# Neighbourhood attention: adding the skewed bias on TensorE inside each unit's scores instead of keeping a masked bias per head

## The chip, the cores and the metric

The kernel is one program on one core of a Trainium2 chip. The metric is the device time of one execution in microseconds (us). The kernel before was timed in three runs: 3856.1 us in the median, from 3851.97 to 3873.37 us.

The program is written out by hand for five engines: TensorE (PE; PEld is its weight load), VectorE (DVE), ScalarE (ACT), GpSimd (POOL) and SyncE (SP), which issues the DMAs here. Each engine runs its own list in order; semaphores tie the lists together.

## The reference, cut to what matters

The whole reference is two transformer blocks over 512 tokens. The change touches one of its parts, the neighbourhood attention of the first block: 8 heads of 64 columns, 512 latent tokens seen as a grid of 8 rows by 64 columns, and 256 context tokens.

```python
bias = rpb[:, dr[:, None, :, None], dc[None, :, None, :]].astype(f32)
s_win = jnp.einsum('brqhd,brkwhd->bhrqkw', qg, k_band) + bias[None]
s_win = jnp.where(col_ok[:, None, :], s_win, NEG_INF)     # a window of 16 grid columns
s_ctx = jnp.einsum('brqhd,bnhd->bhrqn', qg, kc.astype(f32))
s = jnp.concatenate([s_win.reshape(B, NA_H, rows, GRID_W, n_win), s_ctx], axis=-1)
p = jax.nn.softmax(s, axis=-1)
```

`rpb` holds, for each head, 15 x 31 numbers, looked up by the row distance and the column distance of a query and a key.

## The kernel before, in words

The first block runs through a prelude (norms, and `ADA = 4` of 12 pieces of the modulation product `ada_w`), then the neighbourhood attention (`attention_pe`, `attention_act`, `attention_dve`), then the projections of the recurrence (`z_pe`), and so on. Barriers on all compute engines stand before and after the attention.

**Iterations and units.** The attention has four iterations `i`, one for two heads each. An iteration has 8 units `u`: four tiles of 128 queries (16 grid columns by 8 rows) for each of the two heads. A unit's scores are a bank of 512 columns: 256 window keys (8 rows of 32 grid columns) and 256 context keys. They are kept with the sign turned (queries are scaled by -0.125), so that the softmax takes a minimum. TensorE makes the scores of units 2n and 2n+1 together (`heads_scores_pe`, L633), one head in rows 0 to 63 of the array and one in rows 64 to 127. VectorE then adds the bias to the window half and takes the minimum (L767, L769, L771), ScalarE takes the exponentials (L716, L718), TensorE transposes the weights (L669), ScalarE (even units, L725) or VectorE (odd units, L777) copies them out, TensorE multiplies them by the values (L677), VectorE scales (L787), and the tile is turned and stored (L683, L728, L791).

**Work beside the units.** While iteration i runs, the projections of iteration i+1 (`na_prep_pe`, L812: queries, keys, values, from weights W[0], W[1], W[2] of 512 KB each) are cut into steps of two products. `attention_order` calls for three steps at each unit (`a.rate`). The steps are a generator: a bare `yield` is a step without a product on that engine. The end of the key part is the mark "qk"; at the last unit VectorE reorders queries and keys for iteration i+1 (`na_finish_dve`, L978 and L981).

**The bias.** It is read from a padded table in DRAM by `bias_load`: for each head 8 small DMAs (L344) that write a skewed copy, so that row distance and column distance become plain offsets. The skew comes out with its rows reversed; TensorE multiplies it by a reversed identity (`flip`, `na_bias_pe`, L874) into a bank, and VectorE makes from it three forms for each head (L892), with the columns outside the window set to 1e30. `na.bias` keeps 8 heads x 3 forms x 256 columns. The skewed copies have two buffers, `na.skew[i % 2]`.

**SyncE's list.** For each iteration `na_prep_sp` issues in this order: the three weight loads of i (L903), the 16 small DMAs of `bias_load(i + 1)`, and two `ada_w` pieces of 2 MB each, as two DMAs of 1 MB each (L331). GpSimd multiplies and sums these pieces (`ada_rest_pool`, L514 and L519, eight pieces r0 to r7 in all); a piece's buffer is free when the piece two before it is summed (`ada_summed`). A wait in this list holds everything behind it.

Of the kernel before, what the change touches and what calls it, by code (L numbers as in the profile page):

```python
# [11 lines left out]
ALU = mybir.AluOpType  # L12
# [111 lines left out]
def constants():  # L124
# [5 lines left out]
    c["headones"] = np.kron(np.eye(2), np.ones((64, 64)))  # L130
    c["flip"] = np.eye(P)[::-1]

# [27 lines left out]
    for tile in (0, 1, 3):  # L160
        ci = (NA_SPAN * tile + p % NA_SPAN)[:, None]
        cj = NA_FIRST[tile] + np.arange(NA_KEYS)[None, :]
        c0 = np.clip(ci - 8, 0, 48)
        least.append(np.where((cj >= c0) & (cj < c0 + 16), -FAR, FAR))
    c["na_least"] = np.concatenate(least, 1)
# [49 lines left out]
def memory(k, A, PS):  # L215
# [25 lines left out]
    na.skew = [A.take(2, GH * NA_WIDE) for _ in range(2)]  # L241
    na.bias, na.least = A.take(8, 3 * GH * NA_KEYS), A.take(3, NA_KEYS)
    m2 = A.at
# [91 lines left out]
def bias_load(k, p, i):  # L335

    S, na = k.S, k.na
    for x in range(2):
        if i >= 2:
            p.wait_ge(S.bias_filled, 2 * (i - 2) + x)  # L340
        for y in range(GH):
            row = k.scratch[2 * i + x, y:y + GH, 0:NA_WIDE]
            skew = bass.AP(tensor=row.tensor, offset=row.offset + 64 - NA_SPAN, ap=[[1, NA_SPAN], [160, GH], [1, NA_WIDE]])
            p.e.dma_start(na.skew[i % 2][NA_SPAN * y:NA_SPAN * y + NA_SPAN, x].rearrange("p (a b) -> p a b", b=NA_WIDE),  # L344
                          skew).then_inc(*p.up(S.landed(f"bias{i}"), (x, y)))
# [279 lines left out]
def heads_scores_pe(k, p, a, i, units, first):  # L625

    S = k.S
    p.wait_ge(S.qk_ready, (a.name, i))
    for u in (first, first + 1):
        p.claim(("bank", a.scores[u % 2]), S.weights_exp, (a.name, i, u))  # L630
    for j in range(2):
        for u in (first, first + 1):
            ins = p.e.matmul(k.bank[a.scores[u % 2]][:, TC * j:TC * j + TC], units[u][3], units[u][4][j], start=True, stop=True,  # L633
                             skip_group_check=True)
            if j:
                ins.then_inc(*p.up(S.scores_filled, (a.name, i, u)))


def attention_pe(k, p, a):
# [3 lines left out]
    for i in range(a.n):  # L643
        work = Work(a.prep_pe(k, p, a, i + 1) if i + 1 < a.n else None)
        units = a.units(i)
        for step, u in attention_order(a):
# [10 lines left out]
            if step == "values":  # L657
                a.values_pe(k, p, a, i)
                continue
            tile, c0, w, _, _, va, _ = units[u]  # L660
            if step == "scores":
# [71 lines left out]
def attention_dve(k, p, a):  # L733
# [4 lines left out]
    for i in range(a.n):  # L738
        work = Work(a.prep_dve(k, p, a, i + 1) if i + 1 < a.n else None)
        units = a.units(i)  # L740
        for step, u in attention_order(a):
# [13 lines left out]
            if step == "values":  # L755
                continue
            tile, c0, w, _, _, _, bias = units[u]
            cols = a.small[:, u % 4, :]
            low = cols[:, 0:1]
            if step == "scores":  # L760
                s, ps = a.S[u % 2], k.bank[a.scores[u % 2]]
                old = before(a, i, u, 2)
                if old:
                    p.wait_ge(S.weights_filled, old)
                p.in_order()
                p.wait_ge(S.scores_filled, key)
                p.e.tensor_tensor_reduce(out=s[:, 0:TC], in0=ps[:, 0:TC], in1=bias, scale=1.0, scalar=FAR, op0=ALU.add,  # L767
                                         op1=ALU.min, accum_out=low).then_inc(*p.up(S.scores_biased, key))
# [97 lines left out]

def na_bias_pe(k, p, i):

    S, na = k.S, k.na
    p.wait_ge(S.landed(f"bias{i}"), (1, GH - 1))  # L870
    for x in range(2):
        h = 2 * i + x
        p.claim(("bank", 6 + x), S.bias_kept, h)
        p.e.matmul(k.bank[6 + x][:, 0:GH * NA_WIDE], k.K["flip"], na.skew[i % 2][:, x], start=True, stop=True,  # L874
                   skip_group_check=True).then_inc(*p.up(S.bias_filled, h))
        yield
        yield


def na_bias_dve(k, p, i):  # L880

    S, na = k.S, k.na
    for x in range(2):
        h = 2 * i + x
        yield
        yield
        p.wait_ge(S.bias_filled, h)
        skewed = k.bank[6 + x][:, 0:GH * NA_WIDE].rearrange("p (a b) -> p a b", b=NA_WIDE)
        kept = na.bias[:, h].rearrange("p (v a b) -> p v a b", a=GH, b=NA_KEYS)
        for tile in (0, 1, 3):  # L890
            v, at = NA_FORM[tile], NA_FIRST[tile] - NA_SPAN * tile + NA_SPAN
            p.e.scalar_tensor_tensor(out=kept[:, v], in0=skewed[:, :, at:at + NA_KEYS], scalar=-1.0,  # L892
                                     in1=na.least[:, v, None, :].to_broadcast([P, GH, NA_KEYS]), op0=ALU.mult, op1=ALU.max).then_inc(
                                         *(p.up(S.bias_kept, h) if tile == 3 else p.up(S.vector_step)))


NA_COLUMNS = (1152, 1664, 2176)
# [16 lines left out]
def na_prep_pe(k, p, a, i):  # L914
    S = k.S
    for j in range(3):
# [10 lines left out]
        if j == 1:  # L927
            yield from na_bias_pe(k, p, i)
            yield "qk"


def na_prep_act(k, p, a, i):
    S = k.S
    for j, dst in enumerate((a.q_n, a.k_n, a.v_f)):
# [19 lines left out]
        if j == 1:  # L954
            for _ in range(4):
                yield
            yield "qk"


def na_prep_dve(k, p, a, i):  # L960
    S = k.S
    for j in range(3):
# [7 lines left out]
        if j == 1:  # L970
            yield from na_bias_dve(k, p, i)
            yield "qk"
# [11 lines left out]
def na_columns(x, tile):  # L984

    return x.rearrange("p (r c) -> p r c", c=GW)[:, :, NA_FIRST[tile]:NA_FIRST[tile] + NA_KEYS]


# [21 lines left out]
def na_setup(k):  # L1010
# [4 lines left out]
    def units(i):  # L1015
        return [(tile, 64 * h, 64, a.q_s[64 * h:64 * h + 64, tile * P:tile * P + P],
                 [na_columns(a.k_s[64 * h:64 * h + 64, 0:T], tile), a.k_s[64 * h:64 * h + 64, T:TK]],
                 lambda j, h=h, tile=tile: a.v_t[:, 2 * tile + j if j < 2 else 6 + j, 64 * h:64 * h + 64],
                 a.bias[:, 2 * i + h, NA_FORM[tile] * TC:NA_FORM[tile] * TC + TC]) for tile in range(TT) for h in range(2)]
    two_heads(a, units)  # L1020
# [3196 lines left out]
```

## Time and profile before

| | |
|---|---|
| median of three runs | 3856.1 us |
| profiled execution, its own time | 3852.21 us |
| its span in the trace | 3850.4 us |
| PE busy | 3280.3 us, 85% of the span |
| DVE busy | 2121.7 us, 55% |
| POOL busy | 1384.7 us, 36% |
| ACT busy | 764.9 us, 20% |
| DMA moved | 831.77 MB |

The profile page is one execution. The attention stands between about 99 us and 291 us of the span, and the projections for its first iteration between 66 and 99 us. PE records come in two for each product in 32-bit floats, so an x12 is six products; a row of the timeline gives start, length, and in square brackets how long the engine was idle before it and for whom. The granted clock is given as a share of the full one. A transpose and a product both show as MATMUL.

### The profile page before, as it was taken

The page shows a single profiled execution, that of the slowest core. Times are in us where ns is not written, and L with a number is a line of the kernel's source. Part 1 is how long each engine was busy: PE and PEld are TensorE (multiplying, and loading weights), DVE is VectorE, ACT ScalarE, POOL GpSimd, SP SyncE. Part 2 cuts the span into 40 slices and gives each one's busy share as a digit, 9 for nine tenths or more (in the row PEclk, how much of TensorE's full clock was granted, in tenths as well). Part 3 has the DMA queues.
Part 4 walks back from the last instruction along what each step waited for, and adds up shares of the span by engine and source line. Part 5 has one row for each costly group of instructions (what it writes and reads, how often), then busy time and mean ns, then how long its engine had stood idle before and what let it go on. Part 6 is the DMA issues. An engine that isn't in the chain of part 4 may idle for free. (4 is left out here: it accounts for less than half of the span.)

```text
span 3850.4 us, 39434 instructions
## 1 busy us (share of the span) xinstructions
PE 3280.3 (85%) x14438; PEld 2437.0 (63%) x14438; DVE 2121.7 (55%) x4234; ACT 764.9 (20%) x1791; POOL 1384.7 (36%) x1218
## 2 busy tenths in 40 slices
PE   8889888887677978647788888889897999999999
PEld 3566478775233535326567776667785778887787
DVE  2341345548889888867777668776653320133201
ACT  2231233222111111112420012320013210122100
POOL 0930022105677777754355546545500000000000
PEclk9998899998888989878689999889998999999999
DMA  6412100017999999987689999889941134431342
GB/s 206 129 66 82 31 1 1 13 44 275 363 368 373 373 374 384 393 308 276 208 288 376 394 377 371 302 282 392 394 145 34 60 125 150 147 99 61 126 152 100
DMA packets 424598, 831.77 MB, mean 216 GB/s; under 512 B 40467, under 2 KB 266830, under 8 KB 424398
## 3 DMA queue, kind: packets, MB, share of 16 engines
q0 software_dynamic: 147456, 536.94, 37.2%
q1 hardware_dynamic: 276950, 292.31, 23.3%
q8 instruction: 116, 1.90, 0.2%
q14 instruction: 76, 0.62, 0.0%
HBM read 826.98 MB, written 2.17 MB: 215 GB/s over the span
## 5 line engine op out<-in xcount | busy, mean ns | idle before, releaser
L2828 PE MATMUL banks<-arena 128*128 128x256 f32 (+1 forms) x4992 | 1142.4, 388 | 74.4 <-DMA arena<-in_l_w_up 30.4
L2828 PEld LDWEIGHTS banks<-arena 128*128 128x128 f32 (+1 forms) x4992 | 965.4, 195 | 236.8 <-issue 36.2
L2375 POOL DMA_INDIRECT arena<-in_peer_u,arena x512 | 577.6, 1128 | 456.4 <-DVE arena L2505 175.4
L2375 POOL DMA_INDIRECT arena<-in_peer_v,arena x512 | 590.5, 1153 | 400.5 <-DVE arena L2491 242.3
L2505 DVE CUSTOM_DVE_ANT_0 arena<-arena 128x1024 f32<-128x1024 f32 x512 | 628.1, 1227 | 104.4 <-DMA arena<-in_peer_u,arena 86.4
L2447 PE MATMUL banks<-arena 128*128 128x512 f32 x768 | 415.5, 685 | 188.5 <-ACT arena L2466 123.6
L2491 DVE SCALAR_TENSOR_TENSOR arena<-arena 128x1024 f32<-128x1024 f32 x316 | 406.3, 1286 | 29.4 <-DMA arena<-in_peer_v,arena 18.7
L2447 PEld LDWEIGHTS banks<-arena 128*128 128x128 f32 x768 | 159.7, 218 | 401.1 <-issue 246.4
L3737 PE MATMUL banks<-arena 128*128 128x256 f32 x1408 | 310.5, 378 | 0.0
L3786 DVE TENSOR_TENSOR arena<-banks,arena 128x512 f32<-128x512 f32 x44 | 30.5, 692 | 504.9 <-PE banks L2828 504.6
L3737 PEld LDWEIGHTS banks<-arena 128*128 128x128 f32 x1408 | 265.7, 189 | 38.3
L3758 ACT ACTIVATE arena<-banks 128x512 f32<-128x512 f32 x44 | 26.3, 597 | 684.7 <-PE banks L2828 679.7
L3279 DVE CUSTOM_DVE_ANT_0 arena<-banks,arena 128x256 f32<-128x256 f32 (+3 forms) x128 | 59.8, 467 | 138.6 <-PE banks L3161 131.4
L2140 PE MATMUL banks<-arena 128*128 128x512 f32 (+1 forms) x320 | 126.0, 542 | 9.4 <-DMA arena<-in_peer_q_w 5.9
L1632 POOL TENSOR_TENSOR arena<-arena 128x512 f32<-128x512 f32 x48 | 52.4, 1091 | 223.5 <-DVE arena L1598 119.1
L552 PE MATMUL banks<-arena 128*128 128x512 f32 (+1 forms) x336 | 132.1, 553 | 0.0
L812 PE MATMUL banks<-arena 128*128 128x512 f32 (+1 forms) x320 | 120.2, 525 | 5.7 <-ACT arena L455 3.6
L1552 ACT ACTIVATE arena<-banks 128x512 f32<-128x512 f32 x132 | 77.0, 597 | 223.9 <-PE banks L1428 173.2
L3231 ACT ACTIVATE arena<-arena 128x256 f32<-128x256 f32 (+3 forms) x128 | 69.3, 542 | 254.2 <-DVE arena L3279 185.0
L3202 PE MATMUL banks<-arena 128*128 128x64 f32 (+1 forms) x720 | 117.0, 296 | 1.5 <-ACT arena L3249 1.5
L3202 PEld LDWEIGHTS banks<-arena 128*128 128x128 f32 x720 | 111.8, 224 | 4.5 <-issue 2.6
L1435 PE MATMUL banks<-arena 128*128 128x128 f32 x960 | 114.5, 278 | 0.0
(341 smaller groups left out, 3883.7 us busy)
## 6 DMA issues: line engine op xcount, KB each, us to landing
arena<-in_l_w_gate SPq DMA_DIRECT2D x44, 1024.0 KB, 5.5
arena<-in_l_w_up SPq DMA_DIRECT2D x44, 1024.0 KB, 6.1
arena<-in_l_w_down SPq DMA_DIRECT2D x44, 1024.0 KB, 5.1
arena<-in_ada_w SPq DMA_DIRECT2D x24, 1024.0 KB, 7.6
arena<-in_l_w_qkv SPq DMA_DIRECT2D x24, 1024.0 KB, 6.4
arena<-in_w_in SPq DMA_DIRECT2D x33, 512.0 KB, 4.1
arena<-in_l_w_out SPq DMA_DIRECT2D x16, 1024.0 KB, 5.4
arena<-in_peer_q_w SPq DMA_DIRECT2D x10, 1024.0 KB, 12.4
```

Of the source, the lines that this page charges most:

```text
L552: ins = p.e.matmul(k.bank[b][0:m, 0:n], k.W[slot][:, c, 0:m], rhs(c), start=c == 0, stop=c == c_n - 1, skip_group_check=True)
L812: ins = p.e.matmul(k.bank[b][0:m, 0:n], k.W[slot][:, c, 0:m], rhs(c), start=c == 0, stop=c == c_n - 1, skip_group_check=True)
L1435: ins = p.e.matmul(bank[:, s * P:s * P + P], left[:, s, :], right[:, s, :], start=True, stop=True, skip_group_check=True)
L1552: p.e.activation(flat(dst), chunk_bank(k, B, c, step), ACT.Copy).then_inc(*p.up(S.chunk_copied, (c, name)))
L2140: ins = p.e.matmul(k.bank[4][:, cols], ws[:, c, P * j:P * j + P], k.HT[:, c, cols], start=c == 0, stop=c == DC - 1, skip_group_check=True)
L2375: p.e.indirect_dma_start(e.ring[slot], None, tables[table], bass.IndirectOffsetOnAxis(ap=e.IDX[h][:, t, j:j + 1], axis=0)).then_inc(*p.up( ...
L2447: ins = p.e.matmul(k.bank[b], e.diag[x % 4], e.ring[slot][:, half * T:half * T + T], start=h == 0 and j == 0, stop=h == HEADS - 1 and j == ...
L2491: p.e.scalar_tensor_tensor(out=e.ACC[t], in0=e.ring[slot], scalar=factor, in1=e.ACC[t], op0=ALU.mult, op1=ALU.add).then_inc(*p.up(S.rows_a ...
L2505: p.e.tensor_tensor_reduce(out=e.prod, in0=e.ring[slot], in1=e.H2[:, t, :], scale=1.0, scalar=0.0, op0=ALU.mult, op1=ALU.add, accum_out=e. ...
L2828: ins = p.e.matmul(out, left(c), right(c), start=c == 0, stop=c == c_n - 1, skip_group_check=True)
L3202: ins = p.e.matmul(k.bank[5][:, 0:x.w], a.PT[u % 2][:, j * P:j * P + P], values, start=j == 0, stop=j == len(x.values) - 1, skip_group_che ...
L3737: ins = p.e.matmul(k.bank[4 + o // 2][:, o % 2 * TH:o % 2 * TH + TH], w[:, r, P * o:P * o + P], a.hid[:, (i - 1) % 2, TH * r:TH * r + TH], ...
```

## The change

The forms kept for each head go away, with `na_bias_pe` and `na_bias_dve`. The skewed copy is multiplied by the reversed identity once for each unit, and TensorE adds the result in the bank that holds the unit's scores: after the four score products of a pair, two products of 128x256 (L637 of the changed kernel) read the columns of the skew that the tile's form wants. `flip` gets a minus sign since the scores have theirs turned. The first score product of a bank begins it (`start=j == 0`), the flip ends it. What VectorE adds now is a mask of three forms (0 inside the window, 1e30 outside), spread over the 8 rows, the same for all heads; it is loaded as 128 x 768 numbers where 128 x 96 were.

A skewed copy is now read until the last unit of its iteration has its scores, and `bias_load` waits for that.

```diff
@@ bias_load (SyncE)
         if i >= 2:
-            p.wait_ge(S.bias_filled, 2 * (i - 2) + x)
+            p.wait_ge(S.scores_filled, ("na", i - 2, 6 + x))
@@ memory
-    na.bias, na.least = A.take(8, 3 * GH * NA_KEYS), A.take(3, NA_KEYS)
+    na.least = A.take(3, GH * NA_KEYS)
@@ heads_scores_pe
     for j in range(2):
         for u in (first, first + 1):
-            ins = p.e.matmul(k.bank[a.scores[u % 2]][:, TC * j:TC * j + TC], units[u][3], units[u][4][j], start=True, stop=True,
-                             skip_group_check=True)
-            if j:
-                ins.then_inc(*p.up(S.scores_filled, (a.name, i, u)))
+            p.e.matmul(k.bank[a.scores[u % 2]][:, TC * j:TC * j + TC], units[u][3], units[u][4][j], start=j == 0, stop=False,
+                       skip_group_check=True)
+    p.wait_ge(S.landed(f"bias{i}"), (1, GH - 1))
+    for u in (first, first + 1):
+        p.e.matmul(k.bank[a.scores[u % 2]][:, 0:TC], k.K["flip"], units[u][7], start=False, stop=True,
+                   skip_group_check=True).then_inc(*p.up(S.scores_filled, (a.name, i, u)))
@@ na_prep_pe
         if j == 1:
-            yield from na_bias_pe(k, p, i)
             yield "qk"
@@ na_prep_act
-            for _ in range(4):
-                yield
@@ na_prep_dve
-            yield from na_bias_dve(k, p, i)
```

The list of an engine changes in two places that matter here. The first is PE between the third pair of scores of iteration 0 and the first scores of iteration 1. L812 is a projection product, L633 a score product, L874 the flip before; the waits are the semaphores' names. Before:

```order
L633 MATMUL banks<-arena 128x256 x3
L669 MATMUL banks<-arena 128x128 x4
L677 MATMUL banks<-arena 128x64 [waits output_scaled,act_weights]
L677 MATMUL banks<-arena 128x64 x3
L683 MATMUL banks<-arena 128x128
L874 MATMUL banks<-arena 128x384 [waits dve_emptied,landed_bias1]
L874 MATMUL banks<-arena 128x384 [waits dve_emptied]
L669 MATMUL banks<-arena 128x128 [waits weights_exp]
```

and, further on, the last unit with what follows it:

```order
L669 MATMUL banks<-arena 128x128 [waits weights_exp]
L669 MATMUL banks<-arena 128x128 x3
L677 MATMUL banks<-arena 128x64 [waits output_scaled,act_weights]
L677 MATMUL banks<-arena 128x64 x3
L683 MATMUL banks<-arena 128x128 [waits dve_stored]
L812 MATMUL banks<-arena 128x256 x2
L677 MATMUL banks<-arena 128x64 [waits output_scaled,dve_weights]
```

The same last unit in the changed kernel (L671 is the old L669, L679 the old L677, L685 the old L683), and the first scores of iteration 1 with their flips:

```order
L671 MATMUL banks<-arena 128x128 [waits weights_exp]
L671 MATMUL banks<-arena 128x128 x3
L679 MATMUL banks<-arena 128x64 [waits output_scaled,act_weights]
L679 MATMUL banks<-arena 128x64 x3
L685 MATMUL banks<-arena 128x128 [waits dve_stored]
L679 MATMUL banks<-arena 128x64 [waits output_scaled,dve_weights]
L679 MATMUL banks<-arena 128x64 x3
L685 MATMUL banks<-arena 128x128 [waits act_stored,output_scaled]
L633 MATMUL banks<-arena 128x256 [waits qk_ready]
L633 MATMUL banks<-arena 128x256 x3
L637 MATMUL banks<-arena 128x256 [waits landed_bias1]
L637 MATMUL banks<-arena 128x256
```

The four empty or flip steps are gone from the projections, so these come four steps earlier; no projection is left beside the last unit.

The second place is SyncE's list from the weights of iteration 1 to those of iteration 2. Before:

```order
L903 DMA arena<-in_w_in 128x8x128 [waits proj_filled] x3
L344 DMA arena<-rpb_padded 16x8x48 [waits bias_filled]
L344 DMA arena<-rpb_padded 16x8x48 x7
L344 DMA arena<-rpb_padded 16x8x48 [waits bias_filled]
L344 DMA arena<-rpb_padded 16x8x48 x7
L331 DMA arena<-in_ada_w 128x4x512 [waits ada_summed]
L331 DMA arena<-in_ada_w 128x4x512
L331 DMA arena<-in_ada_w 128x4x512 [waits ada_summed]
L331 DMA arena<-in_ada_w 128x4x512
L903 DMA arena<-in_w_in 128x8x128 [waits proj_filled] x3
```

The changed kernel (L875 is the old L903):

```order
L875 DMA arena<-in_w_in 128x8x128 [waits proj_filled] x3
L344 DMA arena<-rpb_padded 16x8x48 [waits scores_filled]
L344 DMA arena<-rpb_padded 16x8x48 x7
L344 DMA arena<-rpb_padded 16x8x48 [waits scores_filled]
L344 DMA arena<-rpb_padded 16x8x48 x7
L331 DMA arena<-in_ada_w 128x4x512 [waits ada_summed]
L331 DMA arena<-in_ada_w 128x4x512
L331 DMA arena<-in_ada_w 128x4x512 [waits ada_summed]
L331 DMA arena<-in_ada_w 128x4x512
L875 DMA arena<-in_w_in 128x8x128 [waits proj_filled] x3
```

The order is the same; what the small DMAs wait for is another signal. The same stands once more an iteration later.

## Rows read from the trace of the kernel before

**Rows 1.** Busy time of each engine in iterations 0 to 3; PEclk, DMA share, GB/s.

```profile
99.50:157.00 57.50, 48.63 (x228) 30.57 (x228) 24.16 (x71) 15.88 (x48) 56.64 (x18) 0.97 0.42 120
157.00:209.00 52.00, 48.31 (x229) 31.09 (x228) 19.40 (x72) 14.59 (x47) 35.42 (x13) 0.97 0.34 107
209.00:260.20 51.20, 46.62 (x227) 29.99 (x226) 19.39 (x72) 14.59 (x47) 30.58 (x10) 1.00 0.33 113
260.20:291.30 31.10, 23.11 (x144) 18.58 (x143) 15.69 (x63) 12.17 (x41) 0.00 (x0) 0.82 0.06 16
```

**Rows 2.** PE by line, 99 to 291 us: busy, mean ns; idle before, for whom.

```profile
L812 PE MATMUL banks<-arena 128*128 128x256 f32 x96 | 23.1, 382 | 0.0
L874 PE MATMUL banks<-arena 128*128 128x384 f32 x12 | 5.2, 512 | 5.4 <-DVE arena L969 5.4
```

**Rows 3.** Timeline of PE, prologue and the passage to iteration 0.

```profile
66.13 20.35 PE L812 MATMUL banks<-arena 128*128 128x512 f32 x48 [3.57 <-ACT arena L455]
86.32 1.66 PE L874 MATMUL banks<-arena 128*128 128x384 f32 x4
88.40 10.58 PE L812 MATMUL banks<-arena 128*128 128x512 f32 x32 [0.42 <-DVE arena L892]
...
155.20 1.08 PE L677 MATMUL banks<-arena 128*128 128x64 f32 x8 [2.89 <-DVE arena L787]
```

**Rows 4.** Timeline of PE in iteration 2.

```profile
208.95 1.14 PE L633 MATMUL banks<-arena 64*128 64x256 f32 x8
...
213.89 5.40 PE L812 MATMUL banks<-arena 128*128 128x512 f32 x12 [0.57 <-ACT arena L836]
...
244.64 1.15 PE L633 MATMUL banks<-arena 64*128 64x256 f32 x8
...
257.66 1.03 PE L812 MATMUL banks<-arena 128*128 128x256 f32 x4
```

**Rows 5.** Timeline of PE in iteration 3, third pair.

```profile
272.83 1.63 PE L633 MATMUL banks<-arena 64*128 64x256 f32 x8 [1.03 <-ACT arena L718]
```

**Rows 6.** Timeline of SyncE's DMA issues, 99 to 164 us.

```profile
99.42 7.79 SPq L344 DMA_DIRECT2D arena<-rpb_padded  x16
115.11 16.42 SPq L331 DMA_DIRECT2D arena<-in_ada_w  x4
131.58 21.13 SPq L903 DMA_DIRECT2D arena<-in_w_in  x3
152.76 8.29 SPq L344 DMA_DIRECT2D arena<-rpb_padded  x16
161.09 2.32 SPq L331 DMA_DIRECT2D arena<-in_ada_w  x4
```

**Rows 7.** L903 alone, 130 to 150 us: two issues, from issue to landing.

```profile
DMA to landing us min/median/max: 8.9/9.4/9.9
```

**Rows 8.** Busy time, clock and DMA of two stretches, columns as in Rows 1.

```profile
163.00:175.60 12.60, 12.60 (x45) 6.24 (x44) 0.76 (x3) 1.59 (x4) 9.29 (x3) 1.00 1.03 368
66.00:72.00 6.00, 5.87 (x7) 2.53 (x8) 0.31 (x1) 2.00 (x5) 0.00 (x0) 0.50 1.05 389
```

**Rows 9.** Timeline of POOL: begin of the sums of r2 and r4, end of r7.

```profile
130.56 7.16 POOL L514 TENSOR_TENSOR arena<-arena 128x2048 f32<-128x2048 f32 x2
...
166.23 7.16 POOL L514 TENSOR_TENSOR arena<-arena 128x2048 f32<-128x2048 f32 x2 [4.26 <-DMA arena<-in_ada_w]
...
237.22 8.31 POOL L519 TENSOR_TENSOR arena<-arena 128x2048 f32<-128x2048 f32 x3
```

**Rows 10.** DVE: duration ns min/median/max, first and last start, of L978 and L981.

```profile
L978 DVE COPY arena<-arena x4: 416/420/2239, 89.2 to 254.1; 128x512 f32<-128x512 f32 x4
L981 DVE COPY arena<-arena x4: 562/564/3842, 89.6 to 254.5; 128x768 f32<-128x768 f32 x4
```

**Rows 11.** Timeline of DVE at the end of iteration 0.

```profile
147.71 2.24 DVE L978 COPY arena<-arena 128x512 f32<-128x512 f32 x1
...
153.74 0.68 DVE L777 COPY arena<-banks 128x512 f32<-128x512 f32 x1
```

More of the change, by code:

```diff
@@ L130, in constants @@
     c["headones"] = np.kron(np.eye(2), np.ones((64, 64)))
-    c["flip"] = np.eye(P)[::-1]
+    c["flip"] = -np.eye(P)[::-1]
     rot = np.zeros((P, P))
@@ L163, in constants @@
         c0 = np.clip(ci - 8, 0, 48)
-        least.append(np.where((cj >= c0) & (cj < c0 + 16), -FAR, FAR))
+        least.append(np.tile(np.where((cj >= c0) & (cj < c0 + 16), 0.0, FAR), (1, GH)))
     c["na_least"] = np.concatenate(least, 1)
@@ L659, in attention_pe @@
                 continue
-            tile, c0, w, _, _, va, _ = units[u]
+            tile, c0, w, _, _, va, _, _ = units[u]
             if step == "scores":
@@ L756, in attention_dve @@
                 continue
-            tile, c0, w, _, _, _, bias = units[u]
+            tile, c0, w, _, _, _, least, _ = units[u]
             cols = a.small[:, u % 4, :]
@@ L766, in attention_dve @@
                 p.wait_ge(S.scores_filled, key)
-                p.e.tensor_tensor_reduce(out=s[:, 0:TC], in0=ps[:, 0:TC], in1=bias, scale=1.0, scalar=FAR, op0=ALU.add,
+                p.e.tensor_tensor_reduce(out=s[:, 0:TC], in0=ps[:, 0:TC], in1=least, scale=1.0, scalar=FAR, op0=ALU.add,
                                          op1=ALU.min, accum_out=low).then_inc(*p.up(S.scores_biased, key))
@@ L861, in rotary_dve @@
     p.e.tensor_tensor(parts[1][0:m, :], k.bank[b][0:m, 0:n], sin[0:m, 0:n], ALU.mult).then_inc(*p.up(k.S.rotated, key))
[L867 to L875, printed above, removed]
-        yield
[L877 to L894, printed above, removed]
 NA_COLUMNS = (1152, 1664, 2176)
@@ L954, in na_prep_act @@
         if j == 1:
-            for _ in range(4):
-                yield
             yield "qk"
@@ L986, in na_columns, with na_skewed @@
     return x.rearrange("p (r c) -> p r c", c=GW)[:, :, NA_FIRST[tile]:NA_FIRST[tile] + NA_KEYS]
+def na_skewed(x, tile):
+    at = NA_FIRST[tile] - NA_SPAN * tile + NA_SPAN
+    return x.rearrange("p (a b) -> p a b", b=NA_WIDE)[:, :, at:at + NA_KEYS]
 NA_VALUES = (7, 6, 7)
@@ L1018, in units @@
                  lambda j, h=h, tile=tile: a.v_t[:, 2 * tile + j if j < 2 else 6 + j, 64 * h:64 * h + 64],
-                 a.bias[:, 2 * i + h, NA_FORM[tile] * TC:NA_FORM[tile] * TC + TC]) for tile in range(TT) for h in range(2)]
+                 a.least[:, NA_FORM[tile], :], na_skewed(a.skew[i % 2][:, h], tile)) for tile in range(TT) for h in range(2)]
     two_heads(a, units)
```

## The prediction

> **What bounds the kernel now.** I read first where the changed lines run, 66 to 291 us, and then the busy time of each engine in the four iterations [rows 1]. In iterations 0 to 2 PE is busy 46.6 to 48.6 us of 51.2 to 57.5 us, VectorE 19.4 to 24.2 us: PE's list sets the pace. In iteration 3, which has no projections beside it, PE is busy 23 of 31 us, and the chain scores, minimum, exponential, transpose sets it. POOL ends its sums at 245.5 us [rows 9], 46 us before the attention does, so it has slack. Barriers stand on both sides, and what follows begins from there, so I count a microsecond in the attention as one in the whole. Next I read the idle times in PE's timeline [rows 3 to 5], and last SyncE's list with its times [rows 6], since the edit of one wait stands there.
>
> **Removed.** In the prologue two flips of 384 columns, 1.66 us, and PE's idle 0.42 us behind the VectorE work on them [rows 3]: -2.1 us. In each of iterations 0 to 2 two flips: 12 records took 5.2 us in all, 1.7 us an iteration, and PE stood idle 5.4 us for VectorE's copy L969 in front of the second, 1.8 us an iteration [rows 2]: -3.5 us. The 24 instructions of L892 stand on VectorE, which isn't the pace; beyond the idle just counted they are worth nothing.
>
> **Added on PE.** 32 flips of 256 columns. The trace has a full product of that size: 96 records, 48 products, 23.1 us, so 0.48 us with its share of the edges, some 0.46 us in a row [rows 2]. A pair of scores takes 1.14 us for four products [rows 4], 0.29 us each, but those run two heads beside each other, and the flip uses all 128 rows. Bounds 0.29 us and 0.83 us (a flip of 384 columns in the prologue, half of 1.66 us [rows 3]); I take 0.46, since that row has the size itself. At the start of an iteration PE waits for the exponentials of unit 0 anyway, and only the first flip is ahead of these: +0.46 us. The other three pairs: +0.92 us each. That is 3.2 us an iteration, against the 3.5 us removed.
>
> At the end of an iteration the projections that filled the last unit are gone (the rows of order above). Before, two of them (1.03 us) stood between the transposes of unit 7 and its output [rows 4]. VectorE's copy of unit 7 takes 0.68 us and stands behind L978 and L981, in the best case 0.98 us together [rows 10, 11]. I get PE waiting about 1.0 us there (0 to 2). So iterations 0 to 2 get -3.5 + 3.2 + 1.0 = +0.7 us each, +2.1 us in all.
>
> In iteration 3 the flips lie on the chain: PE waits 1.0 us for the exponentials (L718) in front of the pair [rows 5]. 0.46 to 0.92 us for the first pair, 0.92 us for the others: +3.4 us.
>
> **The wait that moved.** This is the largest term. Before, `bias_load(2)` found its signal there when SyncE came to it, at 99.42 us [rows 6]. Now it waits for the scores of unit 6 of iteration 0, which come in the fourth pair. Queued behind it are the two `ada_w` pieces and the three weight loads of iteration 2, which PE needs from the first unit of iteration 1. Let F be the time of that signal.
>
> From F: the 16 small issues take about 7.9 us (7.79 and 8.29 us [rows 6]). The next two pieces were 16.4 us apart from first to last issue before, since the second waited for POOL; now both are free, as at 161.09 us, where four issues took 2.3 us. So 4.2 MB go out in a row, with the weights behind them. The trace has that traffic: from 163.0 to 175.6 us, 12.6 us at 368 GB/s, four halves and one weight load issued from 161.09 us on [rows 6, 8]. The DMAs of the weights at 131.58 us, behind 2.1 MB, landed 8.9 to 9.9 us after their issue [rows 7]; 2.1 MB more at 389 GB/s [rows 8] is 5.4 us. Both give about 15 us from the first piece's issue to the landing of W[0]. In sum F + 0.2 + 7.9 + 15.0 = F + 23.1 us.
>
> PE wants W[0] sooner. In iteration 2 the first projection came 4.9 us after the iteration's start and the fourth pair 35.7 us after it [rows 4]. In the changed list six more products of 512 columns (0.90 us each, as the six of 5.40 us [rows 4]) and two of 256 stand ahead of the fourth pair, +6.3 us, the old flips and their wait don't, -3.5 us, and the flips of three pairs do, +2.3 us: the fourth pair at 40.8 us, and after its four products and one flip F at 42.4 us. The iteration ends at 52.0 us (51.3 + 0.7) and the next projection comes 4.9 + 0.46 us later, at 57.4 us: F + 15.0 us. PE stands 23.1 - 15.0, some 8.0 us. It does so in iteration 1 (for the weights of iteration 2) and, the pattern being the same, in iteration 2: +16.0 us. Bounds for one: 5 us (each issue and transfer at its fastest) to 10 us.
>
> A rule of the Trainium skill bears on it. The row first: two weight loads issued behind 2.1 MB took 9.4 us, about what 2.6 MB take plus a start. "DMA: Bandwidth & Descriptors", in "Queues, rings and completion order", says that SyncE owns one row of rings, and that each DMA engine consumes the descriptors of its ring in order. By it the weights can't pass the 4.2 MB, and the stall is 8 us; if they could, it would be none. The trace agrees with the rule.
>
> **The clock.** After PE's idle 3.57 us the granted clock was 0.50 (1.2 GHz of 2.4) from 66 to 72 us with PE busy 5.87 us of 6.0 [rows 3, 8]: that is 3 us of work lost. An idle of 8 us should have at least one such stretch behind it: +3.0 us for each stall (1.7 to 5), +6.0 us.
>
> **VectorE against POOL.** At the end of iteration 0, L978 and L981 took 2.24 and 3.84 us, elsewhere 0.42 and 0.56 us [rows 10, 11]. POOL's sums ran without a break then, and none ran at the end of iteration 2, where POOL was done at 245.5 us, nor at that of iteration 1 (POOL is busy 35.4 of its 52.0 us [rows 1]). PE paid with an idle of 2.89 us [rows 3] and a slower start of iteration 1; the iteration took 57.5 us where its cold start explains 3.1 us over the 51.3 us of iteration 2. I put the price at 3.8 us. In the changed kernel iteration 0 begins at 97.4 us, its F is at 97.4 + 3.1 + 42.4 = 143 us, r2 is issued at 151 us instead of 115.1 [rows 6] and can't be summed before 156 us, while L978 comes at about 149 us and r1's sum ended at 130.6 [rows 9]: POOL is idle there, -3.8 us. But the whole chain of sums moves too. With F now that of iteration 1: r4 lands at F + 13, each sum takes 15.5 us (7.2 + 8.3 [rows 9]), r7 runs from F + 60 to F + 75; iteration 2 begins at F + 10, has a stall and its clock (11 us), and comes to its L978 at F + 69. So the collision comes back there, with less cover on PE: +5.0 us (0 to 7). POOL ends about F + 75, iteration 3 about F + 110, so POOL stays off the path.
>
> The skill's "SBUF — State Buffer", in "Who interferes with whom", says that a VectorE copy in a 2-port mode and a GpSimd instruction exclude each other for the whole instruction. By it L978 waits out whatever instruction POOL has begun, and the price is what the row shows; the trace agrees, and without the rule the +5.0 and -3.8 us would both be nothing.
>
> **The mask.** 344 KB more to load in the prelude, 0.9 us at 389 GB/s, beside PE work that waits for no DMA there: 0 (up to +1).
>
> **The sum.** -2.1 + 2.1 + 3.4 + 16.0 + 6.0 - 3.8 + 5.0 = +26.6 us. The profiled execution took 3852.2 us (its span 3850.4, and 1.8 around it): 3878.8 us. The median of the runs is 3.9 us above that execution, within the scatter of three runs, so I forecast 3879 us.
>
> **The rivals.** *The loads are in time.* If W[0] lands within 15 us of F, because the 16 issues or the transfers are faster than I read, or the weights don't queue behind the pieces, both stalls and their clock go: 26.6 - 22.0 = +4.6, without the collision of iteration 2 about 0: 3852 to 3857 us. Rows 7 speak against it. *Faster than before.* The place is the flip: at 0.29 us instead of 0.46 (what a score product costs in a pair), the 32 give back some 5 us, and with loads in time and no second collision the sum is -5 to -7 us: 3846 us. It decides where PE can put a flip beside a score product of the other head's rows; the full 128 rows speak against it. *The stalls are dearer.* If the clock stays at half for twice the stretch after an idle of 8 us, or the skew of the next iteration lands late as well (it is due at about F + 10.5, its first reader comes at F + 10.9), each stall costs 15 to 18 us: 3890 to 3900 us.
>
> **Chances.** The forecast's mechanism 0.70, by itself 3870 to 3888 us; loads in time 0.17; faster than before 0.04; dearer 0.09. The range that holds 8 in 10 reaches down into the second case and up to the start of the last: 3854 to 3890 us. About 0.5%, 19 us, is what a measurement of this kernel can tell from no change. The forecast lies 23 to 27 us above before, close to that bound, and a fifth of its own case falls within it. Slower by over 0.5%: 0.66. Within: 0.31. Faster by over 0.5%: 0.03.
>
> **What the changed profile would show.** PE idle before the first projection (L814) of iterations 1 and 2, for DMA of the weights, about 8 us each; POOL's r2 starting near 155 us instead of 130.6; SyncE's small DMAs starting at 142 to 143 us instead of 99.4; L637 at 0.46 us each; L946 and L949 (the old L978 and L981) fast at the end of iteration 0, slow at that of iteration 2; the attention ending at about 317 us instead of 291. The prediction is wrong if PE has no such idle, or if later parts of the kernel take the 26 us back.

## The result, and the profile after

The changed kernel took 3881.6 us in the median of 19 runs (3872.96 to 3897.28), the kernel before 3861.9 us in the 19 beside them. The ratio is 1.0058, with a 95% interval from 1.0045 to 1.0071: 17 to 27 us slower. The forecast was 3879 us and the range 3854 to 3890 us. The sum behind it, +26.6 us, stood on one execution of 3852.2 us, 9.7 us under the median that the kernel before shows here.

The profiled execution of the changed kernel took 3891.2 us, its span is 3889.4 us. PE's first product behind the attention (L528) starts at 318.93 us in it, and at 291.29 us in the trace before: the attention ends 27.6 us later. The other 11 us of difference between the two spans lie behind it. That part took 3559.1 us before, 3570.5 us here, and between 3556.9 and 3577.7 us in the ten experiments, whatever they changed in the attention; one execution can't tell more. So below I compare the attention by its traces, and whole kernels by their timed ratios.

Iterations 0 to 3 of the changed kernel, with the columns of [rows 1]:

```profile
97.80:154.90 57.10, 52.14 (x238) 33.55 (x238) 17.11 (x65) 15.89 (x48) 30.55 (x10) 0.94 0.10 23
154.90:218.10 63.20, 52.83 (x240) 34.45 (x239) 17.30 (x66) 14.61 (x47) 30.58 (x10) 0.91 0.34 101
218.10:285.90 67.80, 54.90 (x239) 35.73 (x238) 21.05 (x66) 14.61 (x47) 61.34 (x20) 0.85 0.51 163
285.90:318.90 33.00, 25.85 (x159) 20.61 (x158) 15.68 (x63) 12.07 (x41) 0.00 (x0) 0.86 0.00 1
```

VectorE has some 2 us less to do in an iteration (17.3 us where 19.4 stood), and it gains nothing by it. Iterations 1 and 2, 52.0 and 51.2 us long before, are 63.2 and 67.8 us. The granted clock is lower too: 0.91 and 0.85 where 0.97 and 1.00 stood. SyncE's list, which answers to [rows 6]:

```profile
76.63 21.05 SPq L875 DMA_DIRECT2D arena<-in_w_in  x3
144.63 7.44 SPq L344 DMA_DIRECT2D arena<-rpb_padded  x16
152.12 2.30 SPq L331 DMA_DIRECT2D arena<-in_ada_w  x4
154.46 12.21 SPq L875 DMA_DIRECT2D arena<-in_w_in  x3
207.21 7.68 SPq L344 DMA_DIRECT2D arena<-rpb_padded  x16
214.93 2.33 SPq L331 DMA_DIRECT2D arena<-in_ada_w  x4
217.31 12.18 SPq L875 DMA_DIRECT2D arena<-in_w_in  x3
```

Nothing is issued between 97.7 us and 144.6 us. Before, the same 16 small DMAs went out at 99.4 us. Then all of it comes at once, in two bursts. PE's timeline shows what the weights at the end of each burst do to it:

```profile
154.54 0.48 PE L685 MATMUL banks<-arena 128*128 128x128 f32 x1 [0.45 <-DVE arena L789]
154.95 2.08 PE L633 MATMUL banks<-arena 64*128 64x256 f32 x8
156.96 1.59 PE L637 MATMUL banks<-arena 128*128 128x256 f32 x4
...
168.70 6.82 PE L814 MATMUL banks<-arena 128*128 128x512 f32 x12 [7.37 <-DMA arena<-in_w_in]
...
231.46 7.86 PE L814 MATMUL banks<-arena 128*128 128x512 f32 x12 [6.90 <-DMA arena<-in_w_in]
...
283.15 1.94 PE L679 MATMUL banks<-arena 128*128 128x64 f32 x8 [4.72 <-DVE arena L789]
```

Two idles for the weights, 14.3 us together; behind them six products that take 6.82 and 7.86 us instead of 5.40 us [rows 4]; and an idle of 4.7 us for VectorE at the end of iteration 2, which stood at the end of iteration 0 before (2.89 us [rows 3]). The last is VectorE's copies beside GpSimd's sum of r7 (they took 0.42 and 0.56 us in the median of the same kernel's four). VectorE's timeline, and GpSimd's under it (r4's first instruction and r7's last three):

```profile
277.00 2.15 DVE L946 COPY arena<-arena 128x512 f32<-128x512 f32 x1
279.18 2.58 DVE L949 COPY arena<-arena 128x768 f32<-128x768 f32 x1
```

```profile
220.21 3.60 POOL L514 TENSOR_TENSOR arena<-arena 128x2048 f32<-128x2048 f32 x1 [31.34 <-DMA arena<-in_ada_w]
...
274.33 8.55 POOL L519 TENSOR_TENSOR arena<-arena 128x2048 f32<-128x2048 f32 x3
```

GpSimd waited 31 us for r4 and was still summing r7 when the copies came. The flips themselves cost what a full product of their size costs, 0.38 us a record, two records each (the largest group of the page has 0.39 us). The line's own view, with the duration in ns as least, median and most:

```profile
L637 PE MATMUL banks<-arena x64: 381/381/794, 98.9 to 308.6; 128*128 128x256 f32 x64
```

### The profile page after: what moved, and what is told of

Same layout as the page of the kernel before. It is cut to its first block and busy times, and to the rows that moved or that the text cites. A ratio compares the mean times of both kernels' runs of the same rounds, so it can differ in the third digit from the quotient of the medians.

```text
span 3889.4 us, 39502 instructions
## 1 busy us (share of the span) xinstructions
PE 3299.4 (85%) x14486; PEld 2454.1 (63%) x14486; DVE 2112.2 (54%) x4210; ACT 765.6 (20%) x1791; POOL 1386.9 (36%) x1218
## 5 line engine op out<-in xcount | busy, mean ns | idle before, releaser
L2349 POOL DMA_INDIRECT arena<-in_peer_u,arena x512 | 591.3, 1155 | 455.1 <-DVE arena L2479 163.6
L2349 POOL DMA_INDIRECT arena<-in_peer_v,arena x512 | 579.1, 1131 | 406.5 <-DVE arena L2465 244.2
L814 PE MATMUL banks<-arena 128*128 128x512 f32 (+1 forms) x320 | 124.1, 541 | 18.4 <-DMA arena<-in_w_in 14.3
```

The source lines that it names most:

```text
L814: ins = p.e.matmul(k.bank[b][0:m, 0:n], k.W[slot][:, c, 0:m], rhs(c), start=c == 0, stop=c == c_n - 1, skip_group_check=True)
L2349: p.e.indirect_dma_start(e.ring[slot], None, tables[table], bass.IndirectOffsetOnAxis(ap=e.IDX[h][:, t, j:j + 1], axis=0)).then_inc(*p.up( ...
```

## The experiments

Each table row gives the start of the first scores, the length of iterations 0 to 3 (from scores to scores, the last one to L528) and L528's start, in us. All are one profiled execution; the ratio to before is timed.

| kernel | start | 0 | 1 | 2 | 3 | end | ratio (95%) |
|---|---|---|---|---|---|---|---|
| before | 99.5 | 57.5 | 52.0 | 51.3 | 31.1 | 291.3 | |
| changed | 97.8 | 57.2 | 63.1 | 67.9 | 33.0 | 318.9 | 1.0058 (1.0045 to 1.0071) |
| e1 four skews | 97.3 | 63.0 | 54.6 | 54.2 | 34.1 | 303.1 | 1.0024 (1.0007 to 1.0041) |
| e2 wait only | 100.4 | 54.4 | 57.9 | 61.2 | 30.9 | 304.8 | 1.0026 (1.0013 to 1.0040) |
| e3 weights first | 96.9 | 56.1 | 54.4 | 59.1 | 33.0 | 299.5 | 1.0013 (0.9998 to 1.0027) |
| e4 busy stall | 96.9 | 57.0 | 61.3 | 68.4 | 32.7 | 316.3 | one run, 3882.7 us |
| e5 steps kept | 96.7 | 57.5 | 52.1 | 52.1 | 32.6 | 290.8 | 0.9983 (0.9968 to 0.9998) |
| e6 ScalarE reorders, steps kept | 99.4 | 57.5 | 52.1 | 52.1 | 33.3 | 294.3 | 0.9987 (0.9970 to 1.0004) |
| e7 no flips | 96.6 | 58.5 | 52.2 | 52.2 | 34.7 | 294.1 | 0.9980 (0.9964 to 0.9997) |
| e8 before, ScalarE reorders | 101.8 | 55.6 | 56.0 | 51.3 | 30.3 | 294.9 | 0.9983 (0.9969 to 0.9998) |
| e9 bias later, steps kept | 97.4 | 57.5 | 53.8 | 53.8 | 31.5 | 293.9 | 0.9987 (0.9975 to 0.9999) |
| e10 ScalarE in the loop | 97.6 | 55.2 | 52.1 | 53.8 | 31.6 | 290.1 | 1.0006 (0.9991 to 1.0021) |

The diffs are cut to the lines that matter; of e3, e5, e6, e9 and e10 the rest is said in words. The theory was the prediction's: the moved wait holds back the weights (the stalls and the clock behind them) and shifts GpSimd's sums. The main rival was that the flips on PE are the cost.

**e1, take the wait away.** Four skewed copies, one for each iteration, fit in what the old forms left free.

```diff
-    na.skew = [A.take(2, GH * NA_WIDE) for _ in range(2)]
+    na.skew = [A.take(2, GH * NA_WIDE) for _ in range(4)]
@@ bias_load
-        if i >= 2:
-            p.wait_ge(S.scores_filled, ("na", i - 2, 6 + x))
```

> The changed kernel with a skewed copy for each of the four iterations, so that SyncE's list waits for no scores. Theory (the moved wait holds the weights back): PE has no idle for the DMA of the weights in iterations 1 and 2 (14.3 us less), and its clock doesn't fall there; SyncE's and GpSimd's times are those of the kernel before, so the collision of VectorE's two copies with GpSimd is again at the end of iteration 0, not of iteration 2. The attention ends at 295 to 298 us of the span (291 before, 319 changed); the time is 1.001 to 1.002 of before. Rival (the flips on PE and the emptied last unit are the cost): the attention ends at 310 us or later and the time is 1.005 of before.

The idles for the weights are gone, iterations 1 and 2 are 8.6 and 13.6 us shorter, and the attention ends 15.8 us sooner. That is the theory, and not the rival's 310 us. But the end is 303.1 us, 5 us above the latest that I expected; the ratio, 1.0024, is just above the expected 1.001 to 1.002, which its interval covers. The collision stands again in iteration 0, and it costs more than the kernel before paid, since no projection covers the last unit. VectorE's timeline, then PE's, of this kernel:

```profile
149.09 2.25 DVE L944 COPY arena<-arena 128x512 f32<-128x512 f32 x1
151.38 4.74 DVE L947 COPY arena<-arena 128x768 f32<-128x768 f32 x1
```

```profile
157.50 1.94 PE L677 MATMUL banks<-arena 128*128 128x64 f32 x8 [6.99 <-DVE arena L787]
...
212.92 1.08 PE L677 MATMUL banks<-arena 128*128 128x64 f32 x8 [0.98 <-DVE arena L787]
...
214.85 2.08 PE L631 MATMUL banks<-arena 64*128 64x256 f32 x8
```

The other half of the miss is in the last two lines, from the end of iteration 1 with no collision at all: PE idles 0.98 us, and then the first pair of iteration 2 runs at half the clock (2.08 us for 1.14). Iterations 1 and 2 are 54.4 us, where I had 52.0.

**e2, the wait alone, in the kernel before.**

```diff
@@ bias_load, in the kernel before
-            p.wait_ge(S.bias_filled, 2 * (i - 2) + x)
+            p.wait_ge(S.scores_filled, ("na", i - 2, 6 + x))
```

> The kernel before with one line changed: bias_load waits for the scores of unit 6 and 7 instead of for the old flip. Theory: the stall is the time from that signal F to the landing of the weights (23.1 us by the prediction) less the time from F to PE's first projection of the next iteration. Here the fourth pair comes 35.7 us into an iteration, F at 36.8 us and the next projection at 56.2 us, F + 19.4 us, so the stall is only 3.7 us, with some 2 to 3 us of clock, twice, and the collision with GpSimd moves from iteration 0 to iteration 2. The attention ends at 301 to 306 us. Rival (the wait costs what it costs in the changed kernel, about 22 us, whatever stands ahead of it): 313 us.

SyncE's timeline, then PE's:

```profile
140.30 7.42 SPq L344 DMA_DIRECT2D arena<-rpb_padded  x16
147.77 2.63 SPq L331 DMA_DIRECT2D arena<-in_ada_w  x4
150.44 11.80 SPq L903 DMA_DIRECT2D arena<-in_w_in  x3
```

```profile
164.24 7.46 PE L812 MATMUL banks<-arena 128*128 128x512 f32 x12 [5.14 <-DMA arena<-in_w_in]
...
220.93 8.12 PE L812 MATMUL banks<-arena 128*128 128x512 f32 x12 [3.92 <-DMA arena<-in_w_in]
...
271.08 1.94 PE L677 MATMUL banks<-arena 128*128 128x64 f32 x8 [2.63 <-DVE arena L787]
```

The end at 304.8 us is within what was expected. One line of the diff, alone, makes the kernel slower: 13.5 us in the attention. The idles are 5.1 and 3.9 us (3.7 expected), less than in the changed kernel, because the fourth pair of scores comes sooner in the old order. From the first small DMA to PE's first product with the weights it is 23.9 and 22.7 us here, and 24.1 and 24.3 us in the changed kernel: nearly the same in both, as the theory has it. Iteration 0 is 3.1 us shorter than before and iteration 2 pays the collision instead.

**e3, the same wait, another order behind it.** SyncE issues the three weight loads of iteration i+1 between the small DMAs and the two pieces.

```diff
     if i + 1 < a.n:
         bias_load(k, p, i + 1)
+    if 1 <= i and i + 1 < a.n:
+        na_weights_sp(k, p, i + 1)
     for r in (2 * i, 2 * i + 1):
         ada_rest_sp(k, p, r)
```

> The changed kernel with SyncE issuing the weights of iteration i+1 behind the small DMAs but ahead of the two ada_w pieces. Theory (the weights stand in the queue behind 4.2 MB): they land 0.2 + 7.9 + 4.4 = 12.5 us after F, PE wants them at F + 15, so both stalls go and with them the clock; GpSimd's sums stay late, so the collision stays at the end of iteration 2. The attention ends at 297 to 301 us. Rival (the 16 small issues and the late start are what counts, and the order of the transfers is not): at least half of the 14.3 us of idle stays and the attention ends at 308 us or later.

SyncE's timeline, then PE's:

```profile
142.63 7.44 SPq L344 DMA_DIRECT2D arena<-rpb_padded  x16
150.11 2.69 SPq L875 DMA_DIRECT2D arena<-in_w_in  x3
```

```profile
159.98 5.40 PE L814 MATMUL banks<-arena 128*128 128x512 f32 x12 [0.57 <-ACT arena L838]
...
263.66 1.94 PE L679 MATMUL banks<-arena 128*128 128x64 f32 x8 [4.69 <-DVE arena L789]
```

The end is 299.5 us, as expected. The list still stands until 142.6 us, the 16 small issues still come first, but the weights don't follow 4.2 MB. The first load landed 7.0 us after its issue, 14.5 us after the first small DMA; PE reached it 17.4 us after that DMA and didn't wait. So a stall needs both, the wait and the large transfers between it and the weights. The collision in iteration 2 remains, since GpSimd's pieces are as late as in the changed kernel.

**e4, PE kept busy in the stall.** Eight products more, into the bank of the first projection, ahead of PE's wait for the weights.

```diff
+        if j == 0 and i >= 2:
+            p.claim(("bank", na_bank(0, 0)), S.act_emptied, ("na", i, 0, 0))
+            for x in range(8):
+                p.e.matmul(k.bank[na_bank(0, 0)][:, 0:T], k.ones, k.HT[:, x, :], start=True, stop=True, skip_group_check=True)
         p.wait_ge(S.landed(f"w{j}"), ("na", i))
```

> The changed kernel with 8 products of 128x512 more in iterations 1 and 2, into the bank of the first projection and ahead of PE's wait for the weights; their result is overwritten. They take about 7 us and stand where PE was idle 7.4 and 6.9 us. Theory (the stall costs its length and the clock behind it): the idle falls to under 1 us, the end of the stall doesn't move, and the six products behind it take 5.4 us each time instead of 6.82 and 7.86 us: the attention ends 3 to 4 us sooner, at 315 us. Rival (the clock behind the stall comes from something else, as the wait for VectorE at the end of the iteration): the six products take as long as before and the end stays at 319 us.

PE's timeline; L892 are the products added:

```profile
160.91 7.15 PE L892 MATMUL banks<-arena 128*128 128x512 f32 x16 [0.47 <-ACT arena L838]
167.89 5.32 PE L814 MATMUL banks<-arena 128*128 128x512 f32 x12
...
222.07 7.15 PE L892 MATMUL banks<-arena 128*128 128x512 f32 x16 [0.47 <-ACT arena L838]
229.13 5.43 PE L814 MATMUL banks<-arena 128*128 128x512 f32 x12
```

With PE busy, the six products behind take 5.32 and 5.43 us instead of 6.82 and 7.86: the clock behind the stall is the stall's doing, and it costs 1.5 and 2.4 us, read from one execution. Iteration 1 is 1.8 us shorter, the end 316.3 us (0.9 us of which is the earlier start). It is 1.3 us later than expected; the collision at the end of iteration 2 was worse in this run (an idle of 7.2 us instead of 4.7).

**e5, the emptied unit filled again.** Four skews, and the four bare steps of the old bias work kept in the sequence of projections, on PE, ScalarE and VectorE.

```diff
         if j == 1:
+            for _ in range(4 if i else 0):
+                yield
             yield "qk"
```

> The changed kernel with four skewed copies (no wait for scores) and with the four bare steps of the old bias work kept in the projections' sequence of iterations 1 to 3, on all engines, so that PE again has six plus two products beside unit 7. With the steps gone (the kernel with four skews alone) iterations 1 and 2 took 54.6 and 54.2 us, and PE's clock was at half for 3.4 us at the start of each. Theory (PE's idle at the emptied unit 7 costs its length and brings the clock down): iterations 1 and 2 take 51.5 to 52.5 us, the first pair of scores of iteration 2 takes 1.14 us and not 2.08, and the attention ends at 293 to 296 us. Rival (the clock falls because of the flips themselves): 53.5 us or more, and the first pair stays at 2.08 us.

PE's timeline at the end of iteration 1 and the start of iteration 2:

```profile
203.63 1.03 PE L812 MATMUL banks<-arena 128*128 128x256 f32 x4
204.50 1.00 PE L677 MATMUL banks<-arena 128*128 128x64 f32 x8
...
206.21 1.15 PE L631 MATMUL banks<-arena 64*128 64x256 f32 x8
...
211.79 5.40 PE L812 MATMUL banks<-arena 128*128 128x512 f32 x12 [0.56 <-ACT arena L836]
```

Two products stand again ahead of the last unit's output, PE doesn't idle there, and all first pairs take 1.14 us. Iterations 1 and 2 are 52.1 us, 2.5 and 2.1 us less than in e1; the attention ends at 290.8 us, 12.3 us ahead of e1 and 2 us earlier than I expected. Of the 12.3 us, 5.5 us are iteration 0's, where the two products cover a part of the collision. Against the changed kernel it is 28.1 us shorter in the traces, and the two ratios to before lie 0.75% apart. Against before it can't be called faster: its attention ends only 0.5 us sooner, where the ratio of 0.9983 would ask for 6.6 us. The four kernels timed together, e5 to e8, have ratios from 0.9980 to 0.9987 while their attentions end between 290.8 and 294.9 us, so a part of these ratios is likely the common runs of before, and not the kernels.

**e6, ScalarE reorders queries and keys.** e5 with VectorE's two copies moved to ScalarE (`na_finish_act`), the one before iteration 0 too. e8 is the same edit in the kernel before.

```diff
-    p.e.tensor_copy(a.k_s, a.k_n).then_inc(*p.up(S.qk_ready, ("na", i)))
+    p.e.activation(a.k_s, a.k_n, ACT.Copy).then_inc(*p.up(S.qk_ready, ("na", i)))
```

> As the kernel with four skews and the steps kept, and ScalarE instead of VectorE reorders queries and keys at the end of an iteration, so that no copy of VectorE from SBUF to SBUF stands beside GpSimd's sums. Theory (that collision costs 4 to 7 us wherever it falls): PE has no idle over 1 us for VectorE in front of the outputs of any iteration, iteration 0 takes 53 to 54.5 us, and the attention ends at 287 to 290 us, ahead of the kernel before (291.3). The time is 0.999 of before. Rival (the copies were slow for another reason, as PE's or the DMA's traffic, or ScalarE is later with its own work): ScalarE's copies are slow or delay the exponentials, and the end stays at 293 us or later.

> The kernel before with ScalarE instead of VectorE reordering queries and keys. Theory (the collision of iteration 0 costs the kernel before 3.8 us): iteration 0 takes 53.7 to 54.5 us instead of 57.5, iteration 1 loses its 0.7 us, the attention ends at 287 to 288 us, and the time is 0.999 of before. Rival: ScalarE's copies take 0.6 and 0.9 us on a path that VectorE's took 0.4 and 0.6 us on, and iterations 1 and 2 get longer by a microsecond each, so that the end is at 289 to 290 us.

Both miss, and e6 ends where its rival had it. No long idle for VectorE is left in either, as the theory says, but the first scores come 2.7 and 2.3 us later (ScalarE's two copies of 0.6 and 0.8 us stand in front of them, behind its other work), and in e6 the clock fell once more in iteration 0, so that it took 57.5 us all the same. e8 lost 4 us in iteration 1, where its trace has the clock at half at 162 and 193 us. The ends are 294.3 and 294.9 us. The timed ratio of e8, 0.9983, doesn't show the 3.6 us (0.1%) that its trace lost.

**e7, the price of the flips.** e1 without them; the bias is left out of the scores.

> The kernel with four skews without its flips: the bias is left out of the scores, everything else stays. It prices the 32 products on PE. Theory (PE is the pace, each flip costs its time, 0.99 us for a pair): iterations 1 and 2 take 3.0 to 3.9 us less than 54.6 and 54.2 us, iteration 3 some 3 us less, and the attention ends at 289 to 292 us instead of 303.1. Rival (flips stand where PE waits anyway): less than 5 us in all, 298 us or later.

Iterations 1 and 2 are 2.4 and 2.0 us shorter than in e1, and the end is 294.1 us: 9.0 us for 32 flips, 0.28 us each (0.8 us of the 9.0 is an earlier start, and iteration 0 has 4.4 us of it). It is less than 0.46 us, and less than the 11 to 14 us that I expected. The place where it is missing is iteration 3: without the flips it is 34.7 us, longer than e1's 34.1, and three of its four pairs of scores take 2.08 us, half the clock, where e1 has one. That less work on PE brought this about is my reading; no run tests it. The rival's bound of 5 us is passed, but the flips are not worth their whole time.

**e9, the order of the list instead of the memory.** The changed kernel's two skewed copies and its wait, with the small DMAs of iteration i behind the weights of iteration i, and the steps kept.

```diff
 def na_prep_sp(k, p, a, i):
     ...
-    if i + 1 < a.n:
-        bias_load(k, p, i + 1)
+    if i:
+        bias_load(k, p, i)
```

> The changed kernel with its two skewed copies and its wait for the scores, but the small DMAs of iteration i issued behind the weights of iteration i instead of ahead of them (one place later in SyncE's list), and the four bare steps kept. Theory (it was what stood behind the waiting DMAs that cost, not the wait and not the number of buffers): no idle of PE for the weights, the attention ends within 1.5 us of the kernel with four skews and the steps kept, at 290 to 292 us, and the time is 0.998 to 1.000 of before. Rival (two buffers are too few: the skew lands too late for the first flip of its iteration, or GpSimd's pieces are late again): an idle in front of the flips, or the collision in iteration 2 as well, and an end at 295 us or later.

SyncE's timeline, to be read beside [rows 6]:

```profile
113.00 16.43 SPq L331 DMA_DIRECT2D arena<-in_ada_w  x4
129.47 22.90 SPq L875 DMA_DIRECT2D arena<-in_w_in  x3
152.42 8.73 SPq L344 DMA_DIRECT2D arena<-rpb_padded  x16
161.19 2.53 SPq L331 DMA_DIRECT2D arena<-in_ada_w  x4
```

No stall, neither for weights nor in front of a flip, and SyncE's times are within 2.2 us of those of before: the wait is harmless where nothing urgent stands behind it. The end is 293.9 us, 1.9 us above what I expected: iterations 1 and 2 each had a stretch of half clock (53.8 us instead of 52.1). The ratio is 0.9987.

**e10, ScalarE in the loop only.** e5 with the reordering on ScalarE at the end of iterations 0 to 2, and on VectorE before iteration 0.

> Four skews, the steps kept, and ScalarE reordering queries and keys at the end of iterations 0 to 2 only; before iteration 0 VectorE does it, since ScalarE's two copies put 2 us in front of the first scores when it did that one too. Theory (the collision of VectorE's copies with GpSimd costs iteration 0 some 2.3 us where PE has cover): iteration 0 takes 55 to 55.5 us instead of 57.5, the first scores come at 97 us, and the attention ends at 288 to 289 us, the earliest of all. Rival (iteration 0 is slow for its cold start alone): it takes 57 us or more and the end is at 290.5 us or later.

Iteration 0 is 55.2 us as expected, 2.3 us less than in e5. The collision costs that much where a cover stands, and 6.9 us where none does (e1's iteration 0 against e3's). Iteration 2 met a stretch of half clock from 211.3 us on and took 53.8 us, so the end is 290.1 us instead of 288 to 289. Its line, to be read beside the 5.40 us of e5:

```profile
210.37 7.09 PE L812 MATMUL banks<-arena 128*128 128x512 f32 x12 [0.57 <-ACT arena L836]
```

Its ratio is 1.0006: it can't be told from e5 or from before.

## Why the prediction was right

The lengths of the iterations answer to the terms one by one. Actual against predicted change:

| | predicted | measured |
|---|---|---|
| prologue (earlier start) | -2.1 | -1.7 |
| iteration 0: collision gone, tail and flips | -3.1 + 0.7 = -2.4 | -0.4 |
| iteration 1: stall, clock, tail and flips, less the slow start of before | 8.0 + 3.0 + 0.7 - 0.7 = +11.0 | +11.2 |
| iteration 2: the same and the collision | 8.0 + 3.0 + 0.7 + 5.0 = +16.7 | +16.6 |
| iteration 3: flips on the chain | +3.4 | +1.9 |
| sum | +26.6 | +27.6 |

The time itself is within 3 us of the forecast, and a part of that is luck. The traces have the attention 27.6 us longer, where the sum said 26.6; the timed difference is 17 to 27 us, near whose upper end both lie; and the base of 3852.2 us was 9.7 us low. From the median of 19 runs the same sum would have given 3888.5 us, still in the range but 6.9 us too high.

*The wait that moved.* Right, in place and mechanism (e2 has the wait alone; e3 and e9 keep it and remove its stall by order, e1 takes it away by memory), and the number of skewed buffers was not the matter. Both halves of the difference of 8 us were 1 to 2.5 us too small: the weights came 24.1 and 24.3 us after the first small DMA (22.9 by the sum), PE wanted them 16.7 and 17.4 us after it (14.8), since the iteration's end and its slow start took longer than I had them. The first weight load landed 14.2 us after its issue behind 4.2 MB (changed kernel), and 7.0 us after it ahead of them (e3). The Trainium skill says in "DMA: Bandwidth & Descriptors", "Queues, rings and completion order", that each DMA engine takes the descriptors of a ring in order, and both landings agree with that.

*The clock.* Right as a mechanism (e4), with 1.5 and 2.4 us directly behind the two stalls where I had 3.0. What I missed is that the clock falls elsewhere. The emptied last unit leaves PE idle for only 1 us, as I had it, but the next iteration then begins at half clock. The term "iterations 0 to 2 get +0.7 us each" is the one that was mis-sized: without stall and collision, e1 shows 54.6 and 54.2 us against 51.3, +2.9 to +3.3. Of these, 2.1 to 2.5 us go back when the unit is filled again (e5). The two sizes were off in opposite directions, and so the sum came out closer than its terms, by luck. Iteration 0 has no stall to set against it: -0.4 us instead of -2.4. About half of those 2.0 us stand at its beginning, in a longer stretch of half clock (20.7 us from the first pair of scores to the second, 19.6 us in e1 and e3); e3, with the same wait and list of PE and the shorter stretch, has 56.1 us, -1.4.

*VectorE against GpSimd.* Right: gone at the end of iteration 0, back at that of iteration 2, with an idle of 4.7 us. The +5.0 us for it was near: in e3, which has no stalls, iteration 2 is 4.6 us longer than iteration 1. Its timing was forecast to 1 us (r7 from F + 60 to F + 75, the copies at F + 69). The price depends on cover, 2.3 us with it and 6.9 us without.

*The flips.* 0.38 us a record, a pair 0.99 us in a row, as taken (0.92 us). Iteration 3 grew by 1.9 us instead of 3.4. It isn't the flips' price alone: before, two of its pairs of scores took 1.64 us [rows 5], in the changed kernel the first takes 2.08 us and the others 1.14 us. As in e7, that a busier PE made the difference is a reading and not shown.

*The rivals.* "The loads are in time" is what e3 and e9 built, by an edit; it wasn't this kernel. "Faster than before" needed cheap flips, loads in time and no collision at all; e5 has only the loads in time, and its attention ends 0.5 us before that of the kernel before. "The stalls are dearer" didn't happen.

## What to carry to other kernels

When an edit changes what one instruction in a queue waits for, price what stands behind it, not the wait: here a wait that nobody needed soon held back three weight loads, and 4.2 MB went in front of them when it ended. The repair costs no memory: put the instruction that may wait behind those that are urgent. When work is taken out of a sequence that is dealt out in steps, the steps behind it move up, and the place that they covered may be a dependence that shows only then.

## What the runs showed of the hardware that I had not expected

A short idle can stand in front of half clock. In e1 the granted clock is 1.00 from 168 to 214 us; then, behind an idle of PE of 0.98 us and one of 0.45 us with 1.1 us of work between them, it is 0.50 (1.2 GHz) from 214.4 to 217.8 us. With the last unit covered (e5) the 0.45 us alone, and the idle of 1.48 us behind the first pair of scores, left the clock full in iterations 1 and 2.

The first part of this repeats. In the five kernels with an emptied last unit (changed, e1, e3, e4, e7) 14 of the 15 first pairs of iterations 1 to 3 take 2.08 us. In the seven with a covered one 19 of 21 take 1.14 or 1.15 us, and the other two (1.83 us in before, 2.08 us in e2) stand behind an idle of 2.89 and 2.63 us for VectorE. What comes behind the first pair doesn't repeat: e9 and e10 have the order of PE's list that e5 has and the same idles of 0.45 and 1.48 us around the start of these iterations, and yet some of theirs took 53.8 us with a stretch of half clock behind the first pair, others 52.1 us without one. Those 1.7 us an iteration are as large as several of the effects measured here, and two of the ends missed their expectation by as much.

A flip that reads its moving operand in 8 runs of 32 columns with a step of 48 takes 0.381 us a record in the median, no more than a product that reads 256 columns in a row (0.382 us in the mean [rows 2]).
